# Five products of the eight sample rows with the token weights, computed as partial sums in four column tiles of a PSUM bank and added by VectorE

## The reference

```python
z = jnp.einsum('btd,dp->btp', rms_norm(x, norm_g), w_in)      # D_MODEL = 1024
aq, ak, av, mqk, mv, mg, mo = in_projection(x, ...)           # 512 columns each, mqk has 1024
q = rope(rms_norm(aq.reshape(B, T, H_ATT, HEAD_DIM), qn_g), pos)
k = rope(rms_norm(ak.reshape(B, T, H_ATT, HEAD_DIM), kn_g), pos)
out = (jax.nn.sigmoid(mo.astype(jnp.float32)) * h).astype(mqk.dtype)
```

## Time and profile before

| what | us |
| --- | --- |
| median of 3 executions | 1883.43 |
| lowest, highest | 1868.69, 1888.99 |
| the profiled execution, and its span | 1867.05, 1865.0 |
| TensorE busy in the span | 1826.1 (98%) |
| VectorE busy | 1213.1 (65%) |
| ScalarE busy | 572.8 (31%) |
| GpSimd busy | 496.9 (27%) |
| mean granted TensorE clock | 0.991 of full speed |

### The profile page before, as it was taken

One profiled execution on the slowest core, in us unless ns is written; L12 is line 12 of the kernel. 1 busy time (PEld: TensorE's weight loads), 2 busy tenths in 40 slices (PEclk: granted clock), 3 DMA queues, 4 the chain that ended last, 5 costly groups with the idle time before them and its releaser, 6 DMA issues.

```text
span 1865.0 us, 30861 instructions
## 1 busy us (share of the span) xinstructions
PE 1826.1 (98%) x12689; PEld 1334.9 (72%) x12689; DVE 1213.1 (65%) x2584; ACT 572.8 (31%) x984; POOL 496.9 (27%) x515
## 2 busy tenths in 40 slices
PE   8999999998999999999999999999989999999999
PEld 6743435777888888888888888888855666666665
DVE  7558646455799994665555524344249788788884
ACT  1002122420233323334343333343223333333331
POOL 0001100000065671000000000000077877778740
PEclk9999999898999999999999999999999999999999
DMA  4423622001211333455555565555399999999991
GB/s 165 106 87 109 199 72 101 10 1 71 91 47 51 155 137 137 149 216 227 227 202 201 205 237 204 193 183 188 109 382 383 360 383 378 376 376 380 374 366 63
DMA packets 116812, 368.23 MB, mean 197 GB/s; under 512 B 12105, under 2 KB 72761, under 8 KB 104897
## 3 DMA queue, kind: packets, MB, share of 16 engines
q1 hardware_dynamic: 90992, 291.17, 41.6%
q0 software_dynamic: 25680, 75.10, 11.1%
HBM read 301.35 MB, written 64.88 MB: 196 GB/s over the span
## 4 chain that ended last, share of the span: by engine, by line
PE 86%; DVE 9%; DMA 2%; ACT 1%; SPq 1%; issue 1%; DVEq 0%; ACTq 0%
PE psum L1975 33%; PE psum L2026 24%; PE psum L1690 23%; PE psum L1996 2%; PE psum L1696 1%; PE psum L1781 1%; DVE u_lo L1430 1%; DMA a_in<-d_act 1%; DMA d_w<-w_up 1%; SPq L524 0%; DVE rest L1357 0%; PE psum L1738 0%; DVE ixs L1374 0%; DMA xT<-in_xT 0%; DVE CI L1403 0%
## 5 line engine op out<-in xcount | busy, mean ns | idle before, releaser
L2026 PE MATMUL psum<-w_hl,v_hi 128*128 128x384 bf16 x2048 | 501.0, 327 | 6.0 <-DVE w_hl L1620 6.0
L1975 PE MATMUL psum<-h_hi,u_hi 128*128 128x260 bf16 x2048 | 393.8, 273 | 4.7 <-DVE u_lo L1430 4.0
L1975 PE MATMUL psum<-h_lo,u_hi 128*128 128x260 bf16 x2048 | 393.7, 273 | 0.0
L1975 PE MATMUL psum<-h_hi,u_lo 128*128 128x260 bf16 x2048 | 393.6, 273 | 0.0
L695 POOL DMA_INDIRECT trow<-in_v,t_lists x136 | 173.5, 1275 | 647.8 <-ACT act_f L897 588.1
L2026 PE MATMUL psum<-w_hl,v_lo 128*128 128x384 bf16 x1024 | 334.8, 327 | 0.0
L2026 PEld LDWEIGHTS psum<-w_hl,v_hi 128*128 128x128 bf16 x2048 | 200.8, 98 | 139.1 <-DVE v_lo L1587 6.7
L1430 DVE TENSOR_TENSOR u_lo<-u_raw,u_hi 128x1024 bf16<-128x1024 f32 x128 | 153.8, 1216 | 209.2 <-ACT u_hi L885 209.2
L897 ACT ACTIVATE act_f<-psum 128x520 f32<-128x520 f32 x128 | 77.4, 605 | 467.8 <-PE psum L1975 467.8
L1975 PEld LDWEIGHTS psum<-h_hi,u_hi 128*128 128x128 bf16 x2048 | 195.9, 97 | 34.6 <-DVE u_lo L1430 4.5
L1975 PEld LDWEIGHTS psum<-h_lo,u_hi 128*128 128x128 bf16 x2048 | 198.1, 97 | 30.9
(11 more groups left out here) (372 smaller groups left out, 1867.5 us busy)
## 6 DMA issues: line engine op xcount, KB each, us to landing
u_raw<-in_uT SPq DMA_DIRECT2D x32, 2048.0 KB, 9.7
v_raw<-in_v SPq DMA_DIRECT2D x32, 2048.0 KB, 15.3
wr<-in_w SPq DMA_DIRECT2D x13, 2048.0 KB, 8.0
d_gate<-stage SPq DMA_DIRECT2D x12, 2048.0 KB, 6.3
d_act<-act_f SPq DMA_DIRECT2D x20, 768.0 KB, 3.9
g_in<-d_gate SPq DMA_DIRECT2D x10, 1536.0 KB, 25.0
a_in<-d_act SPq DMA_DIRECT2D x20, 768.0 KB, 16.4
g_up<-d_gate SPq DMA_DIRECT2D x12, 768.0 KB, 9.6
```

Source lines behind the costliest of these rows:

```text
L1975: mm = pe.matmul(upair[n % 2][:, f, 0:HALF], w[g % 2][:, k, c * P:(c + 1) * P], hs[:, k, halves[f]], start=(k == 0 and x == 0), stop=(k == ...
L2026: mm = pe.matmul(ybank[m][:, 0:DENSE], w[g % 2][:, c, m * P:(m + 1) * P], w_hl[g % 2][:, z, c, :], start=(g == 0 and c == 0 and x == 0), s ...
```

## The change

The eight sample rows of each group are computed in four column tiles of a bank. Where two groups share a bank (`qk8`, `vm8`), each has two tiles: one for the first half of the 1024 summed elements, one for the second. The four matmuls of a round go to four different tiles, and there are 4 rounds where there were 8 of two. For mo each tile holds a quarter of the sum, in 2 rounds of four, and the number of matmuls stays 16, 16 and 8. The parts are added while they are taken out of PSUM, by VectorE: four instructions in each of three places. ScalarE loses its two copies of `qk8` and its two of `vm8`, and its sigmoid of the sample rows of mo reads the sum from SBUF after VectorE has released the bank.

```diff
--- before.py
+++ after.py
@@ -734,9 +734,6 @@
             for i in range(NPT):
                 bk = arrived(act, ("q", i))
                 copy(("q", i), zq[:, i, :], bk[:, :])
-            bk = arrived(act, ("qk8",))
-            A(zq[0:DB, NPT, :], bk[0:DB, :], ACT.Copy)
-            copy(("qk8",), zk[0:DB, NPT, :], bk[COLT:COLT + DB, :])
             for i in range(NPT):
                 bk = arrived(act, ("k", i))
                 copy(("k", i), zk[:, i, :], bk[:, :])
@@ -756,14 +753,14 @@
                           scale=token_rms[:, i:i + 1]), ("mv", i))
 
             def output_gate(i):
+                if i == NPT:
+                    emptied(act, ("mo", NPT))
+                    A(sgo[0:DB, NPT, :], sgo[0:DB, NPT, :], ACT.Sigmoid, scale=token_rms[0:DB, NPT:NTT])
+                    return
                 bk = arrived(act, ("mo", i))
                 release(A(sgo[0:rows(i), i, :], bk[0:rows(i), :], ACT.Sigmoid, scale=token_rms[0:rows(i), i:i + 1]),
                         ("mo", i))
 
-            bk = arrived(act, ("vm8",))
-            A(zv[0:DB, NPT, :], bk[0:DB, :], ACT.Copy, scale=token_rms[0:DB, NPT:NTT])
-            release(A(mv1[0:DB, NPT, :, 0:DH], bk[COLT:COLT + DB, :].rearrange("p (h d) -> p h d", h=H), ACT.Copy,
-                      scale=token_rms[0:DB, NPT:NTT]), ("vm8",))
             act.wait_ge(conv_out, CONV_OUT)
             for n, key in enumerate((("sq",), ("sk",))):
                 bk = arrived(act, key)
@@ -1087,7 +1084,14 @@
 
             for g, z, gain in (("q", zq, P_GQ), ("k", zk, P_GK)):
                 for i in range(NTT):
-                    emptied(v, (g, i) if i < NPT else ("qk8",))
+                    if i < NPT:
+                        emptied(v, (g, i))
+                    elif g == "q":
+                        bk = arrived(v, ("qk8",))
+                        do(v.tensor_copy(zq[0:DB, NPT, :], bk[0:DB, :]))
+                        do(tt(zq[0:DB, NPT, :], zq[0:DB, NPT, :], bk[COLT:COLT + DB, :], ALU.add))
+                        do(v.tensor_copy(zk[0:DB, NPT, :], bk[2 * COLT:2 * COLT + DB, :]))
+                        do.release(tt(zk[0:DB, NPT, :], zk[0:DB, NPT, :], bk[3 * COLT:3 * COLT + DB, :], ALU.add), ("qk8",))
                     head_stat(z[0:rows(i), i, :], rt, i)
                 for i in range(NTT):
                     heads = nv[0:rows(i), i * H:(i + 1) * H]
@@ -1099,6 +1103,14 @@
                 for i in range(NTT):
                     rope(z, i, gain)
             do(tt(rt[0:DB, :], zq[0:DB, NPT, :], zk[0:DB, NPT, :], ALU.mult))
+            bk = arrived(v, ("vm8",))
+            of8 = lambda t: bk[t * COLT:t * COLT + DB, :]
+            by_h = lambda x: x.rearrange("p (h d) -> p h d", h=H)
+            rms8, zv8, mv8 = token_rms[0:DB, NPT:NTT], zv[0:DB, NPT, :], mv1[0:DB, NPT, :, 0:DH]
+            do(ts(zv8, of8(0), rms8, None, ALU.mult))
+            do(stt(zv8, of8(1), rms8, zv8, ALU.mult, ALU.add))
+            do(ts(mv8, by_h(of8(2)), rms8, None, ALU.mult))
+            do.release(stt(mv8, by_h(of8(3)), rms8, mv8, ALU.mult, ALU.add), ("vm8",))
             do(v.tensor_reduce(st[0:DB, 184:192], rt[0:DB, :].rearrange("p (h d) -> p h d", h=H), AX.X, ALU.add),
                new_done)
             v.wait_ge(silu_done, 8)
@@ -1160,6 +1172,14 @@
             do(stt(Cs[:, :, :], Ct[:, :, :], gain, Cs[:, :, :], ALU.mult, ALU.add), ms_C)
 
 
+            bk = arrived(v, ("mo", NPT))
+            do(v.tensor_copy(sgo[0:DB, NPT, :], bk[0:DB, :]))
+            for t in range(1, 4):
+                gate = tt(sgo[0:DB, NPT, :], sgo[0:DB, NPT, :], bk[t * COLT:t * COLT + DB, :], ALU.add)
+                if t < 3:
+                    do(gate)
+                else:
+                    do.release(gate, ("mo", NPT))
             v.wait_ge(ms_out, MS_OUT)
 
             def row_max(n):
@@ -1730,23 +1750,25 @@
                 bk = claim(pe, (g, i))
                 product(bk[0:r, :], [(hT[:, k, i * P:i * P + r], w[:, k, :]) for k in range(KT)], (g, i))
 
-            def sample_pair(key, first, second):
-                wa, wb = weights_arrived(pe, first), weights_arrived(pe, second)
+            def sample_tiles(key, groups):
+                w = [weights_arrived(pe, g) for g in groups]
                 bk = claim(pe, key)
-                for k in range(KT):
-                    for at, w in ((0, wa), (COLT, wb)):
-                        mm = pe.matmul(bk[at:at + DB, :], hT[:, k, SEQ:NT], w[:, k, :],
-                                       start=(k == 0), stop=(k == KT - 1), skip_group_check=True)
+                parts = 4 // len(groups)
+                for k in range(KT // parts):
+                    for t in range(4):
+                        part = t % parts * (KT // parts) + k
+                        mm = pe.matmul(bk[COLT * t:COLT * t + DB, :], hT[:, part, SEQ:NT], w[t // parts][:, part, :],
+                                       start=(k == 0), stop=(k == KT // parts - 1), skip_group_check=True)
                 made(mm, key)
 
             for i in range(NPT):
                 token_tile("q", i)
-            sample_pair(("qk8",), "q", "k")
+            sample_tiles(("qk8",), ("q", "k"))
             for i in range(NPT):
                 token_tile("k", i)
             for i in range(NPT):
                 token_tile("v", i)
-            sample_pair(("vm8",), "v", "mv")
+            sample_tiles(("vm8",), ("v", "mv"))
             pe.wait_ge(kscaled, 4)
             for n, key in enumerate((("sq",), ("sk",))):
                 bk = claim(pe, key)
@@ -1783,8 +1805,9 @@
                 if g == 2:
                     mm.then_inc(v_used, 1)
 
-            for i in range(2, NTT):
+            for i in range(2, NPT):
                 token_tile("mo", i)
+            sample_tiles(("mo", NPT), ("mo",))
 
             pe.wait_ge(rope_done, 2 * NTT)
             for i in range(NPT):
```

## The result

The changed kernel took 1886.49 us, a median of 20 executions (1871.13 to 1890.50), and the kernel before 1870.73 us, a median of 20 (1866.41 to 1888.99; the three shown ahead of the prediction were two of its long ones and a short one). The ratio is 1.0067, 95% interval 1.0045 to 1.0089: **0.7% slower, some 12 us**. The forecast was +1.8 us, no change, with a range that holds the time.

A forecast was written before the change was run, and what follows sets the result against it. Chain bound by TensorE to 113 us, VectorE from 114 to 176, then TensorE again; +1.0 (kscaled) + 2.5 (clock) - 5.1 + 2.9 (mo) + 0.5 (clock at scores) = +1.8 us on 1883.4, so 1885 us, range 1869 to 1893.

The forecast's parts named there:

- step 5: After TensorE's wait for kscaled up to 177.1 us: clock falls to half for 5.1 us, 2.5 us lost.
- a sign of being wrong: Behind 260 us: a stage whose length changes by more than a microsecond would show the forecast wrong.
- the same work follows in the same order, and the shift goes through to the end: From 256 us on: later work is unchanged, so the summed +1.8 us reaches the end.
- Step 1: TensorE's column tiles: 0.111 us per 512-column instruction; qk8 and vm8 3.6 us each, sample rows of mo 1.8 us.
- The rival of two streams: Column tiles: four streams run no better than two, so +6.4 us, 1890; chance 10%.
- the serial one: Column tiles: tiles of one accumulation queue behind each other, kernel 24 us slower, 1907; chance 2%.
- Step 2: VectorE's additions in three places: 0.71 us each, 2.84 us per group of four, bounds 2.7 and 3.2.
- Steps 3 and 4: At qk8 and vm8: statistics start 1.8 us earlier, kscaled comes 1.0 us later, TensorE's 6.8 us saving becomes waiting.
- Step 6: Sample rows of mo: TensorE saves 5.1 us, additions cost 2.9; scores start at 256.7 us, 1.2 us late.
- Step 7: At the attention scores: low clock may come sooner and cover more work, 0.5 us lost, bounds 0 and 1.8.
- the clock doesn't fall: Rival at the wait for kscaled: no clock fall, or its loss hidden; -1.2 us, 1882; chance 18%.

The follow-up runs named there:

- e9: Changed kernel with vm8 additions behind kscaled, mv tile 0 ahead of TensorE's wait, sample rows of mo ahead of mo tiles 2 and 3, no filler: 0.9977 of the kernel before.
- e3: Changed kernel with six idle matmuls in TensorE's gaps between the sample rows of mo and the decode values: ratio 1.0014 to the kernel before.
- e6: Changed kernel with ten idle matmuls before kscaled and six between mo and the first decode value: ratio 0.9936 to the kernel before.
- e12: Changed kernel with three idle matmuls in one gap alone, ahead of the first decode value: ratio 0.9981 to the kernel before.
- e5: Changed kernel with ten idle matmuls (8.6 us) behind vm8, in TensorE's wait for kscaled: ratio 1.0009 to the kernel before.
- e4: Kernel before with seven small constant copies on ScalarE ahead of its qT and kT copies, to delay them about 3 us: ratio 1.0007.
- e1: Changed kernel with the sample rows of mo computed as before, sigmoid straight from PSUM: ratio 1.0096 to the kernel before.
- e2: Kernel before with only the sample rows of mo in four column tiles and added by VectorE: ratio 1.0064.
- e13: The changed kernel itself, unedited, measured a second time: ratio 1.0057 to the kernel before.
- e10: Kernel before with one idle matmul behind the last transposed tile and two ahead of the first decode value: ratio 0.9941.

## Why the prediction came out as it did

The range held, but the +1.8 us did not: the change costs 12 us by the ratio. That the forecast median of 1885 us lies so near 1886.49 is luck. The base was 12.7 us too high (1883.4 where 20 executions give 1870.73), and the change some 10 us too small. The steps up to the scores were right in mechanism, and in size but for step 5. The sum was too small because of the clock, at the scores above all. Two of the stages behind 260 us grew by more than a microsecond, which the prediction itself had named as a sign of being wrong; "the same work follows in the same order, and the shift goes through to the end" did not hold.

- **Step 1, the tiles:** right. 0.111 us was forecast for an instruction, 3.62/32 = 0.113 was measured, with four different streams. The rival of two streams and the serial one are out. The share that the Trainium skill gives for three tiles, in "TensorE: Matmul & The Clock Gate", section "Measured speedup vs the span model", would have made it 0.136 us: the trace does not agree.
- **Step 2, the additions:** right. 0.71 us apart in `qk8` and mo, 0.78 with the row scale in `vm8` (3.11 us for four, where 2.84 was taken and 3.2 the bound).
- **Steps 3 and 4:** right to 0.4 us. TensorE's saving of 6.8 us in `qk8` and `vm8` became a wait of 9.17 us (8.8 forecast) that ends at 177.12 (177.1). e9 shows it from the other side: with the additions behind `kscaled` and a useful tile in the gap, the scores start 9.95 us earlier than before.
- **Step 5, the clock after that wait:** the mechanism was right, the size wasn't. It costs 4.6 us (43.63 to 48.23), not 2.5. The clock was already low from 173 us, in the wait, and stayed low until 187, 10 us after the restart and not 5.1. I had counted from the first dense product after the transposes; at half clock the four `qb` instructions took 3.8 us first, and 4.4 us of dense products behind them ran at half clock too.
- **Step 6, mo:** right. -5.1 + 2.9 = -2.2 us was forecast and -2.3 measured.
- **Step 7, the clock at the scores:** this is the step that failed. I took 0.5 us with bounds 0 and 1.8 for the clock at the scores, because the one low stretch there was 3.5 us long and I bounded the new one by its length. It was 30.7 us long, and cost 12.2 us up to `aT`. The low stretch behind `aT`, 6.8 us longer than before, cost another 3.7, for which the sum had no term at all. The bound was wrong in kind: one stretch that ended after 3.4 us doesn't say that the next one will. The high end was half clock for much of the attention's 79.7 us, and the three executions that I had, 20 us apart, were the hint that something of that size comes and goes. e3, e6 and e12 show by removal that the stretch at the scores is the loss: three matmuls ahead of the first decode value take the changed kernel from 1.0057 to 0.9981.
- **The rival "the clock doesn't fall"** would have needed TensorE to work through both gaps. e6 is nearly that kernel, and it is 0.6% faster than before and not only by 1.2 us, since the kernel before has the low stretch too in many executions.
- **The base:** the +1.8 us was set on a median of three that had two long executions in it. The kernel before has two kinds of executions, and the granted clock tells them apart: in the session of e5, 12 lie between 1866 and 1873 us with a mean clock of 0.988 to 0.991, and 19 between 1880 and 1891 us with 0.976 to 0.983. In the measurement of the result 6 of its 20 lie above 1880 us, and 19 of the changed kernel's 20. That is the change's effect on the median, more than any instruction in it.

**What stays open.** What makes the low stretch last 3 us in one execution and 44 in another. The length of the wait ahead alone doesn't tell (e4: 3 us more of it, 10.2 us low and no change in the ratio; e1: the old pace, 20.5 us low), nor does the time at which attention starts (245 to 261 us, long and short). In the profiles of changed, e1, e2, e5, e9 and e13 it was 20 us or longer each time, though the code of the attention is the same as before in all of them. Why these six land there, and the kernel before only in a part of its executions, no run here tells. What happens during it is seen. Two starts of TensorE's scores in the first attention rows, changed kernel:

```profile
264.23 0.79 PE L1710 MATMUL psum<-kT,qT 64*128 64x128 f32 x2
...
267.48 0.79 PE L1710 MATMUL psum<-kT,qT 64*128 64x128 f32 x2
```

and before:

```profile
263.26 0.48 PE L1690 MATMUL psum<-kT,qT 64*128 64x128 f32 x2
...
265.06 0.48 PE L1690 MATMUL psum<-kT,qT 64*128 64x128 f32 x2
```

A round takes 3.25 us at half clock and 1.80 at full, with the same instructions in it, and the clock stays low through some 6 (e1) to 12 (e9) such rounds. Not tried: fillers inside the attention rows, and moving the first decode product, whose wait for VectorE is the gap that e12 filled, behind a few attention rounds.

## What to carry to other kernels

Less work on TensorE is worth nothing ahead of a wait that another engine ends, and costs something if the wait grows so long that the clock falls: move useful work into the gap first (e9), and only then shorten what stands ahead of it. Read the granted clock by stretches of a few microseconds behind each wait, and look at the time of many executions before one profile: where two kinds of executions differ in their mean clock, look for the stretch, and a handful of idle matmuls in the right gap tells in one run what it costs. An addition that takes 3 us is cheap only if nobody's semaphore stands behind it.

## What the runs showed of the hardware

Four column tiles with four different streams of fp32 weights of 512 columns run 3.8 times as fast as one after the other in the full array (0.431 us against 0.113). A TensorE that the profile shows as 98% busy for 44 us may be at half clock for nearly all of it (e9, 248 to 292 us, clock 0.51). And three matmuls of 0.86 us that the result doesn't need, in a wait of 2.6 us that is there anyway, took 13.6 us off the changed kernel (e12 against e13). Three of them, one in the wait ahead of it, took 11 us off the kernel before (e10).
